# State-space layer: when SyncE issues the loads of the four output-weight pieces

## The reference, cut to what matters

```python
def s5_mixer(h, lambda_re, lambda_im, log_step, b_re, b_im, c_re, c_im, d_skip, w_out):
    ...
    bu_re = jnp.einsum('blgc,gpc->blgp', u, bbar_re)
    bu_im = jnp.einsum('blgc,gpc->blgp', u, bbar_im)
    ...
    _, _, x_re, x_im = lax.associative_scan(_complex_affine_combine, (a_re, a_im, bu_re, bu_im), axis=1)
    y = (jnp.einsum('blgp,gcp->blgc', x_re, c_re.astype(jnp.float32))
         - jnp.einsum('blgp,gcp->blgc', x_im, c_im.astype(jnp.float32)))
    y = y.reshape(bsz, s, D_MODEL) + d_skip.astype(jnp.float32) * h32
    y = jax.nn.gelu(y).astype(h.dtype)
    a, g = jnp.split(y @ w_out, 2, axis=-1)
    return a * jax.nn.sigmoid(g)
```

## Time and profile before

| what | value |
|---|---|
| median of three runs | 722.03 us |
| profiled execution, own time / span | 721.63 us / 719.8 us |
| granted TensorE clock, mean | 0.946 |
| PE busy | 629.5 us, 87% |
| DVE, ACT, POOL busy | 27%, 19%, 26% |
| HBM read / written | 239.08 MB / 4.22 MB, 338 GB/s over the span |
| chain that ended last | PE 70%, DMA 20%, SyncE's queue 3%, ACT 2%, issue 2%, DVE 2% |

### The profile page before, as it was taken

One profiled execution on the slowest core, in us unless ns is written; L12 is line 12 of the kernel. 1 busy time (PEld: TensorE's weight loads), 2 busy tenths in 40 slices (PEclk: granted clock), 3 DMA queues, 4 the chain that ended last, 5 costly groups with the idle time before them and its releaser, 6 DMA issues.

```text
span 719.8 us, 13190 instructions
## 1 busy us (share of the span) xinstructions
PE 629.5 (87%) x5567; PEld 401.9 (56%) x5567; DVE 193.5 (27%) x499; ACT 136.6 (19%) x301; POOL 190.5 (26%) x226
## 2 busy tenths in 40 slices
PE   7999998999999988979698978999999699696683
PEld 6888886777456546556263743447554366253240
DVE  3234233256232022102123760226302013002003
ACT  3111313232021012010115511114211012010003
POOL 1001120160599997870861000021000000000001
PEclk9999999999998999989899999999999989898688
DMA  9997976554999999999996529995898999999992
GB/s 314 349 308 160 376 181 223 201 226 183 402 421 419 422 420 421 411 424 421 422 393 272 168 98 351 422 421 208 340 424 342 423 421 416 420 421 421 421 400 83
DMA packets 86706, 244.20 MB, mean 339 GB/s; under 512 B 28052, under 2 KB 56948, under 8 KB 62580
## 3 DMA queue, kind: packets, MB, share of 16 engines
q1 hardware_dynamic: 85188, 237.50, 85.5%
q0 software_dynamic: 1056, 5.24, 1.8%
q10 hardware_dynamic: 400, 0.57, 0.3%
HBM read 239.08 MB, written 4.22 MB: 338 GB/s over the span
## 4 chain that ended last, share of the span: by engine, by line
PE 70%; DMA 20%; SPq 3%; ACT 2%; issue 2%; DVE 2%; POOL 0%; DVEq 0%; POOLq 0%; ACTq 0%
PE ps L1966 11%; DMA ring<-in_moe_w_down 11%; DMA ring<-in_moe_w_up 8%; PE ps L1702 8%; PE ps L2006 7%; PE ps L2247 7%; PE ps L1837 7%; PE ps L2026 4%; PE ps L1705 4%; PE ps L1766 4%; PE ps L1682 3%; PE ps L1833 2%; SPq L469 2%; DMA ring<-in_ssm_w_out 1%; PE ps L1899 1%
## 5 line engine op out<-in xcount | busy, mean ns | idle before, releaser
L1966 PE MATMUL ps<-ring,xg 128*32 128x256 f32 x1904 | 126.5, 406 | 28.7 <-DMA ring<-in_moe_w_up 14.4
L1966 PEld LDWEIGHTS ps<-ring,xg 128*32 128x32 f32 x1904 | 69.9, 117 | 80.8 <-issue 52.3
L2006 PE MATMUL ps<-ring,hidT 128*32 128x512 f32 x488 | 65.3, 655 | 14.1 <-DMA ring<-in_moe_w_down 9.9
L2026 PE MATMUL ps<-y_sb,pickT 128*128 128x512 f32 x128 | 59.5, 605 | 3.2 <-ACT y_sb L1014 1.6
L2247 PE MATMUL ps<-ring,yT 128*128 128x512 f32 x128 | 56.6, 596 | 3.9 <-DMA ring<-in_ssm_w_out 2.4
L1702 PE MATMUL ps<-xnT,ring 128*128 128x256 f32 x256 | 57.8, 382 | 1.3 <-ACT xnT L890 1.0
L847 POOL TENSOR_TENSOR xh<-x,normw 128x1024 f32<-128x1024 f32 x1 | 2.4, 2352 | 213.3 <-DVE x L1417 213.3
L1702 PEld LDWEIGHTS ps<-xnT,ring 128*128 128x128 f32 x256 | 47.8, 190 | 9.3 <-ACT xnT L890 1.2
L1422 DVE TENSOR_TENSOR hid<-sg,ps 128x256 f32<-128x256 f32 (+1 forms) x18 | 7.2, 399 | 166.2 <-ACT sg L987 152.8
L1837 PE MATMUL ps<-pick,xn 128*128 128x256 f32 x192 | 44.0, 382 | 0.0
L2247 PEld LDWEIGHTS ps<-ring,yT 128*128 128x128 f32 x128 | 23.7, 190 | 34.8 <-issue 31.6
(11 more groups left out here) (370 smaller groups left out, 868.5 us busy)
## 6 DMA issues: line engine op xcount, KB each, us to landing
ring<-in_moe_w_up SPq DMA_DIRECT2D x59, 1024.0 KB, 17.9
ring<-in_moe_w_gate SPq DMA_DIRECT2D x59, 1024.0 KB, 15.1
ring<-in_moe_w_down SPq DMA_DIRECT2D x53, 1024.0 KB, 17.0
ring<-in_attn_w_qkv SPq DMA_DIRECT2D x11, 1024.0 KB, 11.8
ring<-in_moe_w_down SPq DMA_DIRECT2D x16, 512.0 KB, 12.5
ring<-in_ssm_w_out SPq DMA_DIRECT2D x8, 1024.0 KB, 10.1
ring<-in_attn_w_o SPq DMA_DIRECT2D x4, 1024.0 KB, 10.5
chunk_inputs<-turned POOLq DMA_DIRECT2D x3, 1024.0 KB, 10.6
```

Source lines behind the costliest of these rows:

```text
L1966: ins = mm(ps[CAP * h:CAP * (h + 1), GUB, F * half:F * (half + 1)], p.xg[:, c, CAP * (ROUND * r + h):CAP * (ROUND * r + h + 1)], w, start= ...
L2006: ins = mm(ps[CAP * h:CAP * (h + 1), DNB + b, :], hidT[:, r, j, CAP * h:CAP * (h + 1)], w, start=(j == 0), stop=(j == FT - 1), tile_positi ...
L2026: ins = mm(ps[:, u, :], p.pickT[rows, r, tt * P:(tt + 1) * P], y_sb[rows, r, 512 * b:512 * (b + 1)], start=(r == 0), stop=(r == p.rounds - 1))
```

## The change

The loads of pieces 0 and 1 move ahead of the wait for the input product: SyncE issues them directly behind the reload of the chunk tables. Pieces 2 and 3 wait for the input product, since they overwrite what it reads, and for `y_done` 1 (the state outputs of the first half) where they waited for `y_done` 2. The wait for `y_done` 2 now stands behind them, ahead of the down weights. What is loaded, into which place and by which transfers stays as it was, and so do all other engines' programs.

```diff
@@ -562,12 +562,13 @@
                     sp.dma_start(dst[:, :, h, :], wout[:, :, h * D + s * WCOL:h * D + (s + 1) * WCOL])\
                       .then_inc(slot_full[s], 16)
 
-            sp.wait_ge(in_done, 4)
             load_wout(0)
             load_wout(1)
-            sp.wait_ge(y_done, 2)
+            sp.wait_ge(in_done, 4)
+            sp.wait_ge(y_done, 1)
             load_wout(2)
             load_wout(3)
+            sp.wait_ge(y_done, 2)
             for s in range(RING):
                 down(1, OCT * group_of(0) + s, s, down_full[s])
             load_ahead(1)
```

## The result

The changed kernel takes 719.81 us (median of 13 runs, 718.54 to 721.49), the kernel before, on the same chips, 724.85 us (13 runs, 721.34 to 731.5). The ratio is 0.993, 95% interval 0.9904 to 0.9955: 5.0 us less by the medians, between 3 and 7 by the interval. The forecast was 716.9 (714.8 to 721.6) with a gain of 5.1. The level is 3 us off because the three runs shown ahead had a median of 722.03 where all thirteen of the same kernel have 724.85; the gain is right. Most striking is the spread: 10 us before, 3 us after.

What follows compares the result with a forecast made beforehand. The prediction took PE's wait for an output-weight piece and an instruction-fetch gap to be on the chain of waits: -2.4 - 2.7 = -5.1 us. 721.63 - 5.1 = 716.5, with the runs' median 0.4 above: 716.9 us, range 714.8 to 721.6.

Steps and rivals of the forecast that it cites:

- Pieces 0 and 1 behind the reload: On q1 from 390.3 to about 402.8 us, an idle stretch; direct gain 0, the reload keeps its landing.
- rival of the shared queue: Reload and pieces share q1, land together at about 402.8; input product 2.8 us late, 719.7 us; chance 0.07.
- The wait for piece 2, -2.4: Before unit 4, PE's 2.38 us wait for an output-weight piece goes, as pieces 2 and 3 are released earlier.
- The fetch stall, -2.7: In `earlier_chunks(0)`, PE's gap after record 35 is an instruction fetch behind pieces 0 and 1; it goes, saving 2.7 us.
- The sum, -5.1: Whole kernel: the wait for piece 2 and the fetch stall together, -2.4 - 2.7 = -5.1 us.
- Handed on whole: Behind unit 4: a gain at 441 us reaches the end whole, since PE's steps release the expert loads.
- The rule of the Trainium skill: PE's instruction fetch: crossing a 16 KiB block is "mostly hidden"; if right, the gap stays and only -2.4 remains.
- The slower rival: Fetches starve in the input product and `earlier_chunks(1)`: +3.3 us, 725.3 us; chance 0.07.
- The order of the reload: On q1, the reload is served first and the pieces then run from 390.3 to about 402.8 us.
- The signs: In the changed profile: no output-weight wait, `earlier_chunks(0)` unbroken, unit 4 prompt, input product at 400.0, output units 5 us sooner.
- the two rivals at 719.6 and 719.7: 719.6: gap in `earlier_chunks` stays or moves, only -2.4, chance 0.25; 719.7: reload shares q1 with the pieces, chance 0.07.

Runs made afterwards that it cites:

- before, empty instructions: Kernel before with 40 empty instructions at the head of PE's program; stretch from input product to end of unit 7 84.4 us, gap 2.22 us; no ratio given.
- first two early: Changed kernel, but pieces 2 and 3 still wait for `y_done` 2; 722.72 us, ratio 0.9954 to the kernel before.
- last two early: Changed kernel, but pieces 0 and 1 again wait for the input product (`in_done` 4); 723.64 us, ratio 0.9981 to the kernel before.
- changed, again: The changed kernel unaltered, run and profiled once more; 719.29 us, ratio 0.9939 to the kernel before.
- all before the states: Changed kernel without the wait for `y_done` 1, so pieces 2 and 3 follow the input product; 722.59 us, ratio 0.9985 to the kernel before.
- stop by semaphore: Changed kernel with PE waiting for a DVE semaphore between the halves of `earlier_chunks(0)`; 723.1 us, ratio 0.9984 to the kernel before.
- piece by piece: Changed kernel with piece 3 behind `y_done` 2 and only piece 2 behind `y_done` 1; 719.49 us, ratio 0.9941 to the kernel before.
- changed, shifted: Changed kernel with three small matmuls behind the regrouping's keep-warm matmuls; 721.55 us, ratio 0.9954 to the kernel before.

## Why the prediction was right

- **Pieces 0 and 1 behind the reload, direct gain 0, order in the queue kept.** Right. The reload landed 9.6 us after its issue. The rival of the shared queue is out.
- **The wait for piece 2, -2.4.** The mechanism was right, the size at the top of what was seen. In five profiles with this wait it is 2.4, 1.8, 1.3, 0.9 and 0.5 us, since the piece takes between 10.2 and 8.4 us to land after its release, and PE asks for it 7.9 us after it. The one profile that I had gave the largest.
- **The fetch stall, -2.7.** Right in mechanism, and shown: the gap follows the load (it is there with pieces 2 and 3 instead of 0 and 1), it moves with the code by the 20 records inserted, and the packet starts 3 us later under the load. As idle time the size was right as well: `earlier_chunks(0)` went from 419.00 - 414.31 = 4.7 us to 2.0. What I left out is the clock. A stretch at 1.2 GHz followed the stop in six of seven profiles and cost from 1.2 us (the 93 records in "before, empty instructions" take 2.77 us where they take 1.56) over 1.7 (8.80 - 7.10 in units 0 and 1) to 3.7.
- **The sum, -5.1.** In the pair of profiles that I compared both terms came out as forecast, 2.7 and 2.4 of the 5.3 us, because the profile I had forecast from is the one without a dip. In the other profile of the kernel before the wait was 0.5 us and the dip cost 1.7, and the stretch was still 84.2: a term too large and one too small cancelled. That was luck, and so in part is the match of the medians (5.0). The halves taken by themselves gave 3.3 us (first two early, for 2.7) and 1.4 (last two early, for 2.4) by their ratios, with intervals too wide to split the gain.
- **Handed on whole.** Right: 5.3 us in the stretch, 5.3 from the input product to the end, 5.0 in the medians.
- **The rule of the Trainium skill.** "Runtime: NRT & Kernel Launch", section on instruction fetch mechanics, calls the cost of crossing a 16 KB block mostly hidden. On an idle queue the profiles agree: in the changed kernel the dense steps cross a block without a gap. Under a load they do not: 2.3 us, and it moved with the block. The measurement decides.
- **The slower rival.** The input product and `earlier_chunks(1)` under load were what could have starved. Neither did, in the changed kernel or its variants. But in the changed kernel's profile the packet around `earlier_chunks(1)` starts at 431.3, 1.2 us into that step, where in the kernel before it starts at 424.8, 4.5 us ahead of it. So a fetch can be late there too; how much room is left was not found.
- **The order of the reload.** 12.3 us from 390.3 end at 402.6 and not at 402.8, so the rival of the shared queue was priced 0.2 us too high. It changes nothing.
- **The signs.** Three came as written: no wait for an output-weight transfer, `earlier_chunks(0)` in one piece of 2.0 us, unit 4 right behind unit 3. The one in absolute times did not: the input product started at 403.48 and not at 400.0, and the output units ended at 482.6 against 484.4, 1.8 us sooner and not 5. I had not seen that what lies ahead drifts by more than the gain.
- **The level.** 716.9 against 719.8 lay in the range, but by its level alone the time is nearer to the two rivals at 719.6 and 719.7; it is the profile that rules them out. The level rests on three runs of a kernel that spreads over 10 us, and that spread belonged in the text. The clock has a part in it: among the 29 runs of the kernel before beside "changed, again" the four above 728 us have a mean granted clock of 0.932 to 0.939, the six below 721.6 one of 0.951 to 0.956.

## What to carry to other kernels

A short "issue" gap of one engine in the middle of a run of small matmuls, at a count that fits no wait in the code, can be an instruction fetch behind data traffic. Check for a packet of the instruction queue a couple of microseconds before its end, compare when it starts in a kernel without the traffic, and put loads into stretches of large matmuls instead. To see whether a gap belongs to the code's position or to the work, insert a few real instructions ahead of it and look whether it moves. Compare a stretch inside the profile rather than absolute times when what lies ahead of it drifts by more than the effect.

## What was unexpected of the hardware

- PE resumes 2.63 to 2.65 us after the start of the 16 KB packet that it lacks, in six profiles.
- Forty empty instructions at the head of PE's program moved neither the gap nor the counts at the packets; 40 real ones moved the gap by exactly their number.
- With the 16 engines full of a data load, the instruction packet started 3 us later than with an idle queue (14.7 to 14.8 us after the input product's start in six profiles, 11.6 to 11.8 in seven).
- A stop of PE of 2.44 us made by a semaphore came with a stretch 5.3 us longer; the other 2.9 us came with a granted clock of 0.77 and 0.64 behind it. The spread of times is wider in most kernels with a stop than without: 10.2, 7.7 and 8.1 us (before, all before the states, stop by semaphore) against 3.0 and 3.7 (changed, piece by piece). It is no clean line, since "first two early" and "changed, shifted" have no stop in this step and spread over 5.3 and 5.7.
